# RWKV-7 recurrence in a two-block kernel: left products across the array in turn with right products near it, and B, K, R and A of the next pair made on GpSimd

## What is computed

```python
def _rwkv7_step(S, inp):
    r, w, k, v, kk, a = inp
    sa = jnp.einsum('dbhij,dbhj->dbhi', S, -kk)
    S = S * w[..., None, :] + sa[..., None] * (kk * a)[..., None, :] + v[..., None] * k[..., None, :]
    y = jnp.einsum('dbhij,dbhj->dbhi', S, r)
    return S, y
```

```python
    S0 = jnp.zeros((N_DIR, B, H, N, N), f32)
    _, ys = lax.scan(_rwkv7_step, S0, seq)
    y = jnp.moveaxis(ys[:, 0] + jnp.flip(ys[:, 1], axis=0), 0, 1)
```

## Time and profile before

| what | us |
|---|---|
| median of three runs | 2883.79 (2883.17 to 2884.23) |
| the profiled execution | 2885.75 |
| its span in the trace | 2883.9 |
| TensorE busy in the span | 2832.7 |
| VectorE busy | 1456.6 |
| ScalarE busy | 1081.3 |
| GpSimd busy | 146.1 |

### The profile page before, as it was taken

How to read it: one execution, slowest core, us unless ns; L and a number is a source line. 1 busy time by engine, 2 the same in 40 slices (tenths; PEclk the granted TensorE clock), 3 DMA queues, 4 the chain that set the end, 5 groups by cost and what they waited for, 6 DMA issues and landing times.

```text
span 2883.9 us, 43564 instructions
## 1 busy us (share of the span) xinstructions
PE 2832.7 (98%) x19606; PEld 2337.1 (81%) x19606; DVE 1456.6 (51%) x1431; ACT 1081.3 (37%) x1176; POOL 146.1 (5%) x74
## 2 busy tenths in 40 slices
PE   9999999999999999999999999999999998999998
PEld 7788778888888888888888888788877886888886
DVE  6676553443455544443364444466657665543432
ACT  5554542222454832222342222442235532332222
POOL 1000010000110010000110000240000000100001
PEclk9999999999999999999999999999999999999999
DMA  4220022223222022233222223322231003222232
GB/s 150 74 77 2 31 88 102 97 93 110 103 100 88 35 73 94 97 102 110 102 88 102 95 95 115 104 83 81 88 125 35 4 6 135 101 96 97 102 102 74
DMA packets 44953, 249.09 MB, mean 86 GB/s; under 512 B 8507, under 2 KB 12347, under 8 KB 17248
## 3 DMA queue, kind: packets, MB, share of 16 engines
q1 hardware_dynamic: 43616, 242.11, 24.6%
q10 hardware_dynamic: 1152, 4.19, 0.4%
HBM read 237.90 MB, written 8.39 MB: 85 GB/s over the span
## 4 chain that ended last, share of the span: by engine, by line
PE 91%; DVE 5%; ACT 3%; issue 1%; DMA 0%; SPq 0%; DVEq 0%; ACTq 0%
PE ps L667 76%; PE ps L2919 4%; PE ps L1515 1%; PE ps L2501 1%; PE ps L2211 1%; PE ps L3979 1%; PE ps L2926 1%; PE ps L2485 1%; PE ps L3962 1%; PE ps L3991 1%; PE ps L2182 0%; DVE wlo L274 0%; PE ps L3097 0%; DVE gdn_conv L1147 0%; ACT whi L268 0%
## 5 line engine op out<-in xcount | busy, mean ns | idle before, releaser
L274 DVE TENSOR_TENSOR wlo<-wraw,whi 128x2048 fp32r<-128x2048 f32 x210 | 486.6, 2317 | 911.5 <-ACT whi L268 907.3
L268 ACT ACTIVATE whi<-wraw 128x2048 fp32r<-128x2048 f32 x210 | 402.1, 1915 | 900.0 <-PE ps L667 900.0
L667 PE MATMUL ps<-ffn_xh,whi 128*128 128x512 f32 x1408 | 549.2, 390 | 0.2 <-DVE wlo L274 0.2
L667 PE MATMUL ps<-ffn_xh,wlo 128*128 128x512 f32 x1408 | 547.8, 389 | 0.0
L667 PE MATMUL ps<-ffn_xl,whi 128*128 128x512 f32 x1408 | 547.8, 389 | 0.0
L667 PEld LDWEIGHTS ps<-ffn_xh,whi 128*128 128x128 f32 x1408 | 264.3, 188 | 56.9 <-DVE wlo L274 1.0
L667 PEld LDWEIGHTS ps<-ffn_xl,whi 128*128 128x128 f32 x1408 | 264.3, 188 | 55.6 <-issue 0.7
L667 PEld LDWEIGHTS ps<-ffn_xh,wlo 128*128 128x128 f32 x1408 | 264.3, 188 | 54.9
L667 PE MATMUL ps<-ffn_uh,whi 128*128 128x512 f32 x704 | 274.1, 389 | 0.0
L667 PE MATMUL ps<-ffn_uh,wlo 128*128 128x512 f32 x704 | 273.9, 389 | 0.0
L667 PE MATMUL ps<-ffn_ul,whi 128*128 128x512 f32 x704 | 273.9, 389 | 0.0
(11 more groups left out here) (524 smaller groups left out, 4446.5 us busy)
## 6 DMA issues: line engine op xcount, KB each, us to landing
wraw<-in_weights SPq DMA_DIRECT2D x211, 1024.0 KB, 4.8
gates_kept<-gates_tmp ACTq DMA_DIRECT2D x8, 512.0 KB, 4.0
mix_gate<-gates_kept SPq DMA_DIRECT2D x8, 512.0 KB, 11.0
h<-in_x SPq DMA_DIRECT2D x4, 512.0 KB, 9.0
mix_y<-hz_kept SPq DMA_DIRECT2D x2, 1024.0 KB, 6.3
out<-out SPq DMA_DIRECT2D x4, 512.0 KB, 3.1
wraw<-in_weights SPq DMA_DIRECT2D x2, 512.0 KB, 7.4
ple_raw<-in_p SPq DMA_DIRECT2D x4, 256.0 KB, 5.1
```

The costliest lines, as they stand in the source:

```text
L268: c.nc.scalar.activation(c.whi[:, j % 2, :], c.wraw[:, j % 2, :], ACT.Copy).then_inc(c.hi_ready, 1)
L274: c.nc.vector.tensor_tensor(c.wlo[:, j % 2, :], c.wraw[:, j % 2, :], c.whi[:, j % 2, :].bitcast(F32), ALU.subtract).then_inc(c.lo_ready, 1)
L667: last = nc.tensor.matmul(pair[:, m, :], a, b, start=opens and n == 0 and wa + xa == 0, stop=closes and n == len(ks) - 1 and wa == 1)
```

## The change

Three things change. First, the levels of the inverse are walked in eleven phases in every second slot, 7, 9, ... 27 (`PHASES`), in place of one product in a slot. Phase m holds left product m (level m//2, direction m%2) and right product m-1, and the matmuls of the two alternate chunk by chunk: phase 0 has a left product alone and phase 10 a right product alone. The results of both are signalled after the whole phase.

Second, left products go through `across` and not `both`, so that the left and the right product of a chunk use different quarters of the array. Y then lies on the other head's partitions, and ScalarE brings it back with two copies of 64 partitions in place of one of 128.

Third, B, K, R and A are made by GpSimd (`pool_prepare`) from the time that kdir and eB are there. VectorE loses those eight operations of each pair; it gains a wait for A ahead of nkk and one for K ahead of kd.

```diff
@@ -2707,6 +2707,7 @@
 SLOTS = 29
+PHASES = range(7, 28, 2)
...
@@ -2874,6 +2875,31 @@
+        for p in range(HP):
+            for d in range(2):
+                self.pool_prepare(pool, p, d)
+
+    def pool_prepare(self, pool, p, d):
+
+        nc, i = self.c.nc, 2 * p + d
+        r, kdir = self.u[:, p, :], self.t3 if d else self.kd
+        near, far = slice(1 - d, 1 - d + C7), slice(d, d + C7)
+        pool.wait_ge(*self.at("kdir", i))
+        pool.wait_ge(*self.at("eB", i))
+        if p >= 2:
+            pool.wait_ge(*self.at("tB", p - 2))
+        nc.gpsimd.tensor_tensor(self.B[p % 2][:, d, :, :], self.chunks(self.av[:, :]), self.eB[:, :, near], ALU.mult)\
+            .then_inc(*self.done("B"))
+        nc.gpsimd.tensor_tensor(self.K[p % 2][:, d, :, :], self.chunks(kdir[:, :]), self.eB[:, :, near], ALU.mult)\
+            .then_inc(*self.done("K"))
+        pool.wait_ge(*self.at("eR", i))
+        pool.wait_ge(*self.ready(p))
+        if p >= 3:
+            pool.wait_ge(*self.at("dS", 8 * (p - 3) + 7))
+        nc.gpsimd.tensor_tensor(self.AR[p % 3][:, d, :, C7:], self.chunks(r), self.eR[:, :, near], ALU.mult)\
+            .then_inc(*self.done("R"))
+        nc.gpsimd.tensor_tensor(self.AR[p % 3][:, d, :, 0:C7], self.chunks(self.nkk[:, :]), self.eR[:, :, far], ALU.mult)\
+            .then_inc(*self.done("A"))
@@ -2977,17 +3003,11 @@
-        elif 7 <= s < 26:
-            l, what = divmod(s - 7, 4)
-            if what < 2:
-                self.pe_left(pe, k, l, what)
-            else:
-                self.pe_right(pe, k, l, what - 2)
+        elif s in PHASES:
+            self.pe_phase(pe, k, (s - 7) // 2)
         elif s == 26:
...
-        elif s == 27:
-            self.pe_right(pe, k, LEVELS - 1, 1)
@@ -3026,26 +3046,48 @@
+    def lefts(self, m):
+
+        return divmod(m, 2) if m < 2 * LEVELS else None
+
+    def rights(self, m):
+
+        return divmod(m - 1, 2) if m else None
+
+    def pe_phase(self, pe, k, m):
+        left, right = self.lefts(m), self.rights(m)
+        if left is not None:
+            self.left_ready(pe, k, *left)
+        if right is not None:
+            self.right_ready(pe, k, *right)
+        for n in range(NCH):
+            if left is not None:
+                last_left = self.pe_left(n, *left)
+            if right is not None:
+                last_right = self.pe_right(k, n, *right)
+        if left is not None:
+            last_left.then_inc(*self.done("Y"))
+        if right is not None:
+            last_right.then_inc(*self.done("Z"))
...
-        for n in range(NCH):
-            last = self.both(lambda r: out[r, n, :], lambda r: self.LT[r, d, n, :], lambda r: self.X[r, d, n, :])
-        last.then_inc(*self.done("Y"))
...
+    def pe_left(self, n, l, d):
+        out = self.bank(self.y_bank(d))
+        return self.across(lambda r: out[r, n, :], lambda r: self.LT[r, d, n, :], lambda r: self.X[r, d, n, :])
...
@@ -3193,7 +3235,10 @@
-        self.c.nc.scalar.activation(self.Y[:, d, :, :], self.bank(self.y_bank(d)), ACT.Copy).then_inc(*self.done("Yc"))
+        low, high = self.halves()
+        made = self.bank(self.y_bank(d))
+        self.c.nc.scalar.activation(self.Y[low, d, :, :], made[high], ACT.Copy)
+        self.c.nc.scalar.activation(self.Y[high, d, :, :], made[low], ACT.Copy).then_inc(*self.done("Yc"))
@@ -3392,6 +3434,8 @@
         elif s == 4:
             dve.wait_ge(*self.at("rs", p))
+            if p:
+                dve.wait_ge(*self.at("A", 2 * p - 1))
...
@@ -3413,38 +3457,8 @@
-        if s in (10, 19):
...
-            nc.vector.tensor_tensor(self.B[b][:, d, :, :], self.chunks(self.av[:, :]), eB, ALU.mult)\
-                .then_inc(*self.done("B"))
-        if s in (11, 20):
...
-        if s in (12, 22):
...
-        if s in (13, 24):
...
         if s == 25:
+            dve.wait_ge(*self.at("K", 2 * p + 1))
             nc.vector.tensor_tensor(self.kd[:, :], self.kd[:, :], self.t3[:, :], ALU.add).then_inc(*self.done("kd"))
```

More of the change, by code:

```diff
@@ L2764, in __init__ @@
                                         "Kt Bt", "US", "ysq ylog yrs gc yhi")),
[1 row of a table removed]
+                               ("dve", ("neg", "eye", "floor nkk", "scan b kdir", "kd bonus1",
                                         "XTi PT Xi", "MQ", "ys", "X", "XT", "Zs", "ST", "y",
                                         "sum mean centred var normed bonus2 lnw plus out ylo")),
-                               ("pool", ("resets",))):
+                               ("pool", ("resets", "B K R A"))):
             for names in cycles:
@@ L3027, in pe_values, with left_ready @@
         last.then_inc(*self.done("MV"))
[L3029 to L3032, removed]
+    def lefts(self, m):
[17 more added lines that the diff above has]
+            last_right.then_inc(*self.done("Z"))
+    def left_ready(self, pe, k, l, d):
         if l:
@@ L3036, in pe_left @@
         else:
+            pe.wait_ge(*self.at("LT", 2 * k + d))
             pe.wait_ge(*self.at("Xi", 2 * k + d))
@@ L3042, in pe_left, with right_ready @@
                 pe.wait_ge(*self.at("Yc", 10 * k - 2))
-        for n in range(NCH):
-            last = self.both(lambda r: out[r, n, :], lambda r: self.LT[r, d, n, :], lambda r: self.X[r, d, n, :])
-        last.then_inc(*self.done("Y"))
-    def pe_right(self, pe, k, l, d):
-        bank, XT = self.z_bank(l, d), self.XT[k % 2]
+    def pe_left(self, n, l, d):
+        out = self.bank(self.y_bank(d))
+        return self.across(lambda r: out[r, n, :], lambda r: self.LT[r, d, n, :], lambda r: self.X[r, d, n, :])
+    def right_ready(self, pe, k, l, d):
         pe.wait_ge(*self.at("Yc", 10 * k + 2 * l + d))
@@ L3059, in pe_right @@
                 pe.wait_ge(*self.at("ys", k))
[L3060 to L3067, removed]
+    def pe_right(self, k, n, l, d):
+        bank, XT = self.z_bank(l, d), self.XT[k % 2]
+        if l < LEVELS - 1:
+            return self.both(lambda r: self.columns(self.halved(bank)[r, n, :], l),
+                             lambda r: XT[r, d, n, :], lambda r: self.side(self.Y[r, d, n, :], l, d))
+        return self.both(lambda r: self.columns(self.halved(bank)[r, n, :], l), lambda r: self.Y[r, d, n, :],
+                         lambda r: self.side(XT[r, d, n, :], l, 1 - d))
     def pe_turn(self, pe, src, banks, name):
@@ L3180, in act_build @@
                     .then_inc(*self.done("ysc"))
-        if 7 <= s < 26 and (s - 7) % 4 < 2:
-            self.act_left(act, k, *divmod(s - 7, 4))
+        if s in PHASES and self.lefts((s - 7) // 2) is not None:
+            self.act_left(act, k, *self.lefts((s - 7) // 2))
         elif s in (26, 28):
@@ L3361, in dve_build @@
                 .then_inc(*self.done("ys"))
[L3362 to L3366, removed]
+        if s in PHASES and self.rights((s - 7) // 2) is not None:
+            self.dve_right(dve, k, *self.rights((s - 7) // 2))
         if s == SLOTS - 1:
```

25 lines of the change are left out of this document (removed), and 1 row of the table put.

## The result

The changed kernel takes 2898.62 us in the median of 4 runs (2898.18 to 2899.58), the kernel before 2884.01 beside it: ratio 1.0048, 95% interval 1.0036 to 1.0061. It is slower by 0.5%, 14.6 us; forecast were 2883.5, with a range up to 2893. The profiled execution has a span of 2896.4 us, 12.5 more than before.

The account below looks back on a forecast made before the run. TensorE's work was taken to bound the four stretches before, and waits behind each phase after. 2.9 - 0.85 - 2.3 + 0 = -0.25 us gave about 2883.5 us as a median; range 2872 to 2893, the forecast's own 2877 to 2890.

Parts of the forecast that it names:

- the term of pair 0: Inverse levels of pair 0, which has no step between phases: 31.15 us against 28.25, so +2.9, late taps included.
- D hops: From one phase's start to the next with no step between, bound by two Y copies: 2.35 us.
- a rival of 0.14: TensorE's clock falls to 1.2 GHz, in pair 0 and the last hops of pairs 1 to 3: 2893 us, chance 0.14.
- The work of a phase: A phase's two products, 64 records in different quarters: results after 1.15 us, TensorE free after 0.95.
- The rival in which the alternation does nothing: A phase's two products run one after the other, 0.86 us more in each of 36 phases: 2914 us, chance 0.04.
- E: Hop with tK between a pair's last two phases, its 64 records beside the phase's work: 2.8 us.
- C at level 0: Hop with z and U between phases, at level 0, where VectorE's insertion takes 0.74 us: 3.7 us.
- the first hop of a pair: From phase 0, a left product alone, to phase 1: 2.3 us.
- Pairs 1 to 3: Stretches of 31.1, 32.8 and 31.05 us: changes of -0.85, -2.3 and 0.
- the price of nothing: B, K, R and A on GpSimd, 1.29 us each: no time added, neither by lateness nor by holding VectorE up.
- The chains overlap better: Only Y copies bind, 2.35 us a hop, 16.4 us less over pairs 1 to 3: 2867 us, chance 0.25.
- C hops: Hops with z and U between phases, Zs standing behind the transpose: 3.4 us; under 2.8 would favour better overlap.

Follow-up runs that it names:

- e5_pair0_old: Changed kernel with pair 0 in the old order (left products near, one copy of Y, left and right products apart); 2886.9 us, ratio 1.0005.
- e4_near: Changed kernel with left products near again and one copy of Y for all 128 partitions, phases kept; 2909.0 us, ratio 1.0080.
- e13: Changed kernel with TensorE waiting for the copy of Y once and last, in phases with both products from the fourth on; 2896.4 us, ratio 1.0035.
- e8_filled_later: Changed kernel with 16 more TensorE products behind each of pair 0's phases from 2 to 8; 2892.9 us, ratio 1.0028.
- e15: Changed kernel with 16 more TensorE products behind each of phases 0 to 8 of pair 0; 2895.3 us, ratio 1.0030.
- e1: Kernel before with only B, K, R and A made on GpSimd; 2884.7 us, ratio 0.9997.
- e2: Changed kernel with B, K, R and A back on VectorE in their old slots; 2898.3 us, ratio 1.0042.
- e11_both_again: Changed kernel with pair 0 in old order, Y copies of 32 columns and X's transpose one slot later in pairs 1 to 3, measured again; 2881.4 us, 0.9988.
- e16: Changed kernel with pair 0 in old order, Y copies of 32 columns, later transpose, and the copy waited for last in all phases; 2879.4 us, 0.9981.
- e9_turn_later: Changed kernel with pair 0 in old order, Y copies of 32 columns and X's transpose one slot later in pairs 1 to 3; 2881.2 us, 0.9987.

## Why the prediction was wrong

The step that failed is the term of pair 0, +2.9 us in the sum for +10.4 measured. It took D hops of 2.35 us where the chain needs 2.63, and it kept TensorE's clock at its full level, with the fall set apart as a rival of 0.14; the runs show a granted clock of 0.65 there. In the old order in pair 0 (`e5_pair0_old`) 11.8 of the 14.6 us are gone. The rest comes mostly from the same two errors in pairs 1 to 3. Term by term:

- **The work of a phase: right.** 1.15 us for 64 records, and TensorE busy for 73 to 80% of the stretches. The rival in which the alternation does nothing is out: `e4_near` takes 2.06. I had rested that rival on the rule of the Trainium skill (TensorEngine Tiling (Array Packing), "Gotcha 1: PSUM Pressure"), and wrongly: the rule is about row tiles that access one bank, and the two products of a phase write two different banks. So neither the 1.15 nor the 2.06 tests it; one bank is shared only by the two heads of a product, in both kernels alike.
- **The step D: mis-sized, 2.35 for 2.63.** Two errors. I put the second copy 0.48 behind the first, as the next operation stands behind a copy in the earlier trace rows; it came 0.61 behind. And "0.05 us for a signal" is 0.25 from a copy to TensorE; the 0.05 was read from single steps. By e13 0.11 of the 0.2 is the order of the waits; the rest is open. That a copy of half the partitions is as long as a full one (0.59) was right. E was right (2.86 for 2.8), C at level 0 a little long (3.49 for 3.7), the first hop of a pair short (2.85 for 2.3; three more waits stand behind the copy there).
- **Pairs 1 to 3: the sum was 0.9 to 1.1 low each** where the clock stays full: 31.99, 33.69 and 32.10 in `e8_filled_later` for 31.1, 32.8 and 31.05. The changed kernel's own pair 3 took 33.60 at the full clock. Some 0.8 of those 1.5 us lie in three phases that stop inside (1.74, 1.42 and 1.62 us long for 1.52, 1.29 and 1.14); why is open.
- **Pair 0: 31.15 forecast, 35.1 at the full clock (e15), 38.63 in fact.** In e15 the first nine hops take 27.4 us for 24.55; each was forecast too short, most by 0.1 to 0.5 and the first by 0.7. The hop to the last right product takes 3.5 for 2.85, the end with the late taps 4.2 for 3.75, but these two hold the stops of 0.5 and 0.8.
- **The clock: the right rival, with too small a chance.** It named the mechanism, the place (pair 0, and the last hops of pair 1) and the test: the granted clock of pair 0's stretch comes out under 1; it is 0.65. The working failed in keeping it apart from the forecast. It isn't another way for the chains to go but follows from them: the D hop of the forecast itself left TensorE 1.15 us of work in 2.35, the real one 1.15 in 2.63, not far from the 1.26 in 3 ahead of the fall in the earlier trace rows. I had set against it a single stretch in which the clock stayed. More such stretches exist (last section), but the mean clock came out lower in all four executions. Its price for each phase at the lower level was overdone, 1.15 us for 0.82; it is worth 3.5 us or somewhat more in pair 0, and 2.6 in pair 1.
- **GpSimd: the price of nothing was right**, by e1 and e2, and 1.18 us an operation for the 1.29 taken. The reading of the earlier trace rows held, that insertions and transposes aren't stretched. But not all of VectorE's work beside the groups is of that kind, and somebody did wait: in pair 0's preparation VectorE waited 3.83 us for K, and its addition took 1.67 us in place of 0.68. There the rule of the Trainium skill (SBUF — State Buffer, "Who interferes with whom") shows, that a VectorE instruction with two inputs in SBUF contends with a GpSimd one that reads SBUF. It cost nothing because the recurrence did not wait for it (it starts 0.2 us sooner). VectorE's 1.6 us of relief in pair 0 I had not counted.
- **"The chains overlap better": wrong.** It needed C hops under 2.8; they were 3.4. But what it needed can be made in places: with the transpose behind ST and Zs some of these hops come to 2.6 or 2.7 (pair 3 of `e11_both_again`).

Altogether the stretches took 140.8 us for the 126.1 that my four add up to: 6.8 by hops mis-sized (35.1 + 32.0 + 33.7 + 32.1 less 126.1; 1.3 of it are e15's stops), 6.1 by the lower clock, and 1.8 in pairs 2 and 3 that differ between executions.

## What to carry to other kernels

When work is taken off an engine that is busy 94 to 97% of the time, write down the chain that then binds, hop by hop, and price every hop's start with the wait that stands last in that very place, not with the shortest signal in the trace. Hold TensorE's work in your own new hops against the stretches ahead of its clock's falls in the trace: where they look alike, the lower clock belongs in the sum, at its price times its chance, even if a stretch alike can be found in which the clock stayed. Where the new order is right only in some places (here pairs 1 to 3, not pair 0), give it to those alone; with the copy cut to what is read, the operations that others wait for ahead of those that can wait, and the late wait last, a change that lost 0.5% became one that gains 0.26%.

## What was not expected of the hardware

- Satisfied waits behind the releasing one cost TensorE time: 0.47 us from a copy's end to the next matmul with three behind it, 0.25 with one, 0.14 with none (e13); with all three gone the 0.47 became 0.29 (e16).
- Whether the clock falls can't be told from TensorE's work in the stretch ahead. From 2193.4 to 2196.8 TensorE worked 1.60 us in the changed kernel, and the clock fell behind it; with 1.60 it stayed in `e15_filled_from_start`. Even one kernel does both: `e9_turn_later` and `e11_both_again` are the same kernel, and in the first the clock fell (windows of e9, then of e11):

```profile
2193.40:2196.80 3.40, 1.80 (x18) 0.70 (x14) 1.24 (x3) 2.65 (x5) 0.00 (x0) 1.00 0.01 2
2196.80:2200.20 3.40, 3.20 (x121) 3.23 (x125) 2.93 (x5) 1.15 (x3) 0.00 (x0) 0.54 0.03 5
...
2193.40:2196.80 3.40, 1.60 (x19) 0.53 (x16) 1.52 (x3) 2.37 (x5) 0.00 (x0) 1.00 0.00 0
2196.80:2200.20 3.40, 2.93 (x130) 2.26 (x130) 3.40 (x6) 1.83 (x4) 0.00 (x0) 1.00 0.02 5
```

- TensorE sometimes stops inside a product for 0.2 to 1.1 us with nothing to wait for that the profile shows ("issue"): 1.6 us from 2206 to 2400 before and in the changed kernel, 4.2 in `e9_turn_later` and 5.9 in `e11_both_again`, the same kernel. Its cause wasn't tried.
- Two ScalarE copies of 64 partitions, from the two halves of one bank, start 0.61 us apart and don't overlap (each takes 0.59); behind a copy of 128 partitions the next operation starts 0.48 after it.
